# Two streams of 256 columns at the ends of a feed-forward stage

## The reference

```python
for l in range(DEPTH):
    h = x * (1 + sc1) + sh1
    hc = xc * (1 + sc1c) + sh1c
    y, yc = _token_mixers(h, hc, ...)          # attention; ends in "@ w_out"
    x = _layer_norm(ALPHA * x + g1 * y, ln1_g[l], ln1_b[l])
    h = x * (1 + sc2) + sh2
    x = _layer_norm(ALPHA * x + g2 * _sq_relu_mlp(h, w_fc1[l], w_fc2[l]), ln2_g[l], ln2_b[l])
    if not last:
        # the same three lines for the context: xc, yc, g1c, g2c ...
```

## Time and profile before

| | us |
|---|---|
| median of 3 runs (2049.69 to 2050.71) | 2050.25 |
| the profiled execution's own time | 2044.91 |
| its span, first to last instruction | 2043.1 |
| PE busy | 1857.0 |
| DVE busy | 1123.4 |
| mean granted TensorE clock | 0.958 |

### The profile page before, as it was taken

The page is one execution under the profiler, slowest core; times in us unless marked ns, Lnnn a source line. Parts: engine busy times, 40 slices in busy tenths (PEclk is TensorE's granted clock), DMA queues, the critical chain, the costliest instruction groups (busy, mean ns, idle before and its releaser), DMA issues.

```text
span 2043.1 us, 24319 instructions
## 1 busy us (share of the span) xinstructions
PE 1857.0 (91%) x9816; PEld 1322.5 (65%) x9816; DVE 1123.4 (55%) x1848; ACT 761.8 (37%) x1206; POOL 112.7 (6%) x152
## 2 busy tenths in 40 slices
PE   6998799999899899999988887999999788889996
PEld 5655555555576554557635556888888574579996
DVE  5662533323445422337457646788776765756665
ACT  2163333423242433334256534323222424645443
POOL 0770000000000000000000002000000100010000
PEclk9989899999999999999989998999999898989998
DMA  9778499999557899993210021354454031024440
GB/s 368 303 281 319 171 417 398 412 399 371 234 191 281 331 417 422 421 419 119 83 42 1 12 72 51 135 206 178 194 206 178 29 124 42 1 88 175 173 144 21
DMA packets 61848, 430.15 MB, mean 211 GB/s; under 512 B 6560, under 2 KB 9760, under 8 KB 9888
## 3 DMA queue, kind: packets, MB, share of 16 engines
q1 hardware_dynamic: 61728, 428.51, 53.0%
HBM read 427.43 MB, written 1.05 MB: 210 GB/s over the span
## 4 chain that ended last, share of the span: by engine, by line
PE 71%; DVE 17%; ACT 9%; issue 2%; DMA 0%; DVEq 0%; SPq 0%; POOL 0%; ACTq 0%
PE bank L293 14%; PE bank L1141 10%; PE bank L297 9%; PE bank L298 9%; PE bank L299 9%; PE bank L1129 7%; DVE ring_halves L2466 3%; ACT work_halves L2460 2%; PE bank L332 2%; ACT work_halves L1061 2%; DVE ring_halves L1068 2%; PE bank L2139 1%; PE bank L2116 1%; DVE work L439 1%; PE bank L2487 1%
## 5 line engine op out<-in xcount | busy, mean ns | idle before, releaser
L297 PE MATMUL bank<-work_halves 128*128 128x512 f32 (+1 forms) x1344 | 473.5, 352 | 37.9 <-DVE ring_halves L2466 12.1
L299 PE MATMUL bank<-work_halves,ring_halves 128*128 128x512 f32 (+1 forms) x1344 | 461.7, 343 | 0.0
L297 PEld LDWEIGHTS bank<-work_halves 128*128 128x128 f32 x1344 | 259.1, 193 | 76.3 <-DVE ring_halves L2466 15.1
L298 PE MATMUL bank<-HH_halves,work_halves 128*128 128x512 f32 (+1 forms) x832 | 289.8, 348 | 0.0
L299 PEld LDWEIGHTS bank<-work_halves,ring_halves 128*128 128x128 f32 x1344 | 258.8, 193 | 28.9
L1141 PE MATMUL bank<-ring,work 128*64 128x512 f32 x1024 | 261.2, 598 | 0.4 <-ACT work_halves L1324 0.4
L2466 DVE TENSOR_TENSOR ring_halves<-ring,work_halves 128x2048 fp32r<-128x2048 f32 x72 | 164.7, 2288 | 48.3 <-ACT work_halves L2460 48.3
L298 PEld LDWEIGHTS bank<-HH_halves,work_halves 128*128 128x128 f32 x832 | 162.2, 195 | 20.5 <-issue 2.2
L293 PE MATMUL bank<-HH,ring 128*128 128x256 f32 x704 | 160.2, 387 | 13.2 <-DVE HH L518 6.6
L298 PE MATMUL bank<-work_halves 128*128 128x512 f32 (+1 forms) x512 | 172.0, 336 | 0.0
L293 PEld LDWEIGHTS bank<-HH,ring 128*128 128x128 f32 x704 | 135.3, 194 | 42.5 <-issue 13.8
(11 more groups left out here) (322 smaller groups left out, 2629.7 us busy)
## 6 DMA issues: line engine op xcount, KB each, us to landing
ring<-in_ws_dram SPq DMA_DIRECT2D x380, 1024.0 KB, 7.3
work<-in_ws_dram SPq DMA_DIRECT2D x24, 1024.0 KB, 9.5
con<-in_con_dram SPq DMA_DIRECT2D x1, 1204.0 KB, 25.1
XX<-in_xT_dram SPq DMA_DIRECT2D x1, 1024.0 KB, 9.9
XX<-in_cT_dram SPq DMA_DIRECT2D x1, 1024.0 KB, 15.5
out_dram<-XX SPq DMA_DIRECT2D x1, 1024.0 KB, 4.8
par<-in_par_dram SPq DMA_DIRECT2D x1, 338.0 KB, 3.0
con<-in_con_dram SPq DMA_DIRECT2D x1, 128.0 KB, 2.9
```

Source lines behind the costliest of these rows:

```text
L297: pe.matmul(out, l[0], r[0], start=start, stop=False)
L298: pe.matmul(out, l[0], r[1], start=False, stop=False)
L299: return pe.matmul(out, l[1], r[0], start=False, stop=stop)
```

## The change

The 512 columns of layer 0's feed-forward stage are handled as two streams of 256 (the number q, 0 for the tokens and 1 for the context) at both ends of the stage. In the output projection PE runs all eight products for stream 0, then all eight for stream 1, and the norm of stream 0 is spread between the steps of stream 1 on ACT, DVE and PE. Fc1 0 (`pe_first`) runs over stream 0, then the variance matmuls of stream 1, then stream 1. Fc2 7 (`pe_last`) runs eight products for stream 0 and eight for stream 1, with the norm of stream 0 begun in between, and waits for both of its weight chunks before the first product. The first projection of layer 1's mixer runs over stream 0, then does the variance matmuls of stream 1, then runs over stream 1. The fourth weight chunk gets a buffer of its own, the evictions four buffers of 256 columns, and one buffer of the next mixer is placed elsewhere so that both of its first splits come at step 34. Layer 1's stage (one stream) goes through the same functions.

```diff
 class Mix:                                   # __init__
-    after = work[:, WORK - 2 * CW:WORK - CW]
+    after = work[:, 13312:13312 + CW] if self.last else work[:, WORK - 2 * CW:WORK - CW]
...
     def pe_proj(self, pe, *tiles):
...
-        for k in range(8):
-            for b, (name, w, m, n) in zip(bs, tiles):
-                for q in range(n // 256):
-                    st.wait_ge(pe, "xl", k, q)
...
+        streams = ((0, 1), (1, 2)) if self.before and len(tiles) > 1 else ((0, 2),)
+        for q0, q1 in streams:
+            if q0 > 0:
+                self.before.pe_norm(pe, 1, 1)
+            for k in range(8):
+                for b, (name, w, m, n) in zip(bs, tiles):
+                    x = slice(256 * q0, min(n, 256 * q1))
+                    if x.start >= n:
+                        continue
+                    for q in range(q0, x.stop // 256):
+                        st.wait_ge(pe, "xl", k, q)
...
+                    t = mm3(pe, b[:, x], (wh[:, k, c], wl[:, k, c]), (xh[:, k, x], xl[:, k, x]), k == 0, k == 7)
...
 class Ffn:
-    self.tmp = [work[:, 5120 + 512 * i:5632 + 512 * i] for i in range(2)]
+    self.tmp = [work[:, 5120 + 256 * i:5376 + 256 * i] for i in range(4)]
+    self.extra = work[:, 6144:8192]
...
+    def high_of(self, i):
+        return self.extra if i == 3 and self.nq == 2 else self.buf[i % 3]
...
+    def pe_norm(self, pe, v, q):
...
+        for k in range(0, 8, 2):
+            st.wait_ge(pe, "dev", v, q, k)
+            t = pe.matmul(b[:, 0:256], ones, self.dev[:, k, self.half(q)], start=k == 0, stop=k == 6)
...
+    def pe_sums(self, pe, v, q, o):
+        if o < 2 and q > 0:
+            self.pe_sum(pe, v, q - 1, 6 + o)
+        if o >= 2:
+            self.pe_sum(pe, v, q, o - 2)
+        if o == 7 and q == self.nq - 1:
+            self.pe_sum(pe, v, q, 6)
+            self.pe_sum(pe, v, q, 7)

     def pe(self, pe):
+        for q in range(self.nq):
+            for o in range(8):
...
+                b = bank_of(pe, st, self.ro, "out", q, o)
+                st.wait_ge(pe, "low", j)
+                for k in range(8):
+                    st.wait_ge(pe, "ol", k)
+                    t = mm3(pe, b[:, 0:256], (wh[:, k, c], wl[:, k, c]), (oh[:, k, x], ol[:, k, x]), k == 0, k == 7)
...
+                self.pe_sums(pe, 0, q, o)
+                if q > 0 and o == 4:
+                    self.pe_norm(pe, 0, 0)
...
-                    self.pe_fc1(pe, 0, (0, 1), i)
+                    self.pe_first(pe, i)
...
+                elif f < 7:
                     self.pe_fc2(pe, f, j, i)
+                elif j == 0:
+                    st.wait_ge(pe, "low", i + 1)
+                    self.pe_last(pe, i)
...
+    def pe_first(self, pe, i):
+        tiles = [(j, m, bank_of(pe, st, self.ro, "fc1", 0, 2 * j + m)) for j in range(2) for m in range(2)]
+        for q in range(self.nq):
+            if q > 0:
+                self.pe_norm(pe, 0, 1)
+            for k in range(8):
+                st.wait_ge(pe, "xl", k, q)
+                for j, m, b in tiles:
...
+    def pe_last(self, pe, i):
+        for q in range(self.nq):
+            for o in range(8):
+                b = bank_of(pe, st, self.ro, "fc2", 7, q, o)
+                for k in range(4):
...
+                self.pe_sums(pe, 1, q, o)
+                if q > 0 and o == 5:
+                    self.pe_norm(pe, 1, 0)

     def act(self, act):                      # after the first stream's eight act_out
+        if self.nq == 2:
+            for o in range(8):
+                self.act_out(act, 1, o)
+                if o < 2:
+                    self.act_squares(act, 0, 0, range(4 * o, 4 * o + 4))
+                if o == 4:
+                    self.act_root(act, 0, 0)
+                    self.split_act(act, 4)
+                if o == 6:
+                    self.split_act(act, 5)
+                if o >= 5:
+                    self.act_rows(act, 0, ((0, 1), (2, 3), (4, 5, 6, 7))[o - 5])
+        q = self.nq - 1
+        self.act_squares(act, 0, q, range(8))
...
+        self.act_root(act, 0, q)
+        self.act_rows(act, q, range(8))
...
-            if self.next and i >= 34:
-                st.wait_ge(act, "used", self.w[i - 1])
-                self.next.split_act(act, i - 34)
+            if self.next and i == 34:
+                st.wait_ge(act, "used", self.w[33])
+                self.next.split_act(act, 0)
+                self.next.split_act(act, 1)
...
+        for q in range(self.nq):
+            self.act_squares(act, 1, q, range(8))
+            self.act_root(act, 1, q)
+            for k in range(8):
+                st.wait_ge(act, "normed", 1, q, k)
+                if self.next:
                     self.next.high_x(act, k, q)
+                act.activation(XX[:, k, c], XX[:, k, c], ACT.Identity, ...)

     def dve(self, dve):
+        self.dve_mean(dve, 0, 0)             # mean and eight subtractions of stream 0
+        if self.nq == 2:
+            self.dve_out(dve, 1, (0, 1))
+            self.dve_pairs(dve, 0, 0)
+            self.dve_out(dve, 1, (2, 3, 4))
+            self.dve_root(dve, 0, 0)
+            self.dve_rows(dve, 0, (0, 1))
+            self.split_dve(dve, 4)
+            self.dve_out(dve, 1, (5,))
+            self.dve_rows(dve, 0, (2, 3))
+            self.dve_out(dve, 1, (6,))
+            self.dve_rows(dve, 0, (4, 5))
+            self.split_dve(dve, 5)
+            self.dve_out(dve, 1, (7,))
+            self.dve_rows(dve, 0, (6, 7))
+            self.dve_mean(dve, 0, 1)
...
+        for o in range(8):
+            self.dve_last(dve, 0, o)
+            if self.next and o in (1, 3):
+                self.next.split_dve(dve, o // 2)
+        self.dve_mean(dve, 1, 0)
+        if self.nq == 2:
+            for o in range(3):
+                self.dve_last(dve, 1, o)
+        self.dve_pairs(dve, 1, 0)
+        if self.nq == 2:
+            for o in range(3, 8):
+                self.dve_last(dve, 1, o)
+        for q in range(self.nq):
+            if q > 0:
+                self.dve_mean(dve, 1, q)
+                self.dve_pairs(dve, 1, q)
+            self.dve_root(dve, 1, q)
+            for k in range(8):
+                dve.tensor_tensor(XX[:, k, c], XX[:, k, c], self.rs[:, c], MUL)...
+                if self.next:
+                    self.next.dve_h(dve, k, q)
+                    if k > 0 and q == 0:
+                        self.next.low_x(dve, self.next.st.dve, k - 1, 0)
...
     def pool(self, pool):
+        for q in range(self.nq):
+            for k in range(8):
+                c = slice(512 * k + 256 * q, 512 * k + 256 * q + 256)
...
```

More of the change, by code:

```diff
@@ L2437, in plan @@
                 ro = self.ro = Rota(list(range(6)))
-                for o in range(8):
-                    ro.take("out", o)
-                    if o % 2:
-                        self.feed()
-                ro.take("var", 0)
+                for q in range(self.nq):
+                    for o in range(8):
+                        ro.take("out", q, o)
+                        if q == 0 and o % 2:
+                            self.feed()
+                for q in range(self.nq):
+                    ro.take("var", 0, q)
                 s = 0
@@ L2445, in plan @@
                     for j in range(2):
-                        for m in range(2 if name == "fc1" else 4):
-                            ro.take(name, f, 2 * j + m if name == "fc1" else 4 * j + m)
+                        if (name, f) == ("fc2", 7):
+                            if j == 0:
+                                for q in range(self.nq):
+                                    for o in range(8):
+                                        ro.take("fc2", 7, q, o)
+                        else:
+                            for m in range(2 if name == "fc1" else 4):
+                                ro.take(name, f, 2 * j + m if name == "fc1" else 4 * j + m)
                         self.feed()
@@ L2481, in pe_sum @@
-            def pe_sum(self, pe, v, o):
-                if o >= 0:
-                    st, n = self.st, self.n
-                    st.wait_ge(pe, "res", v, o)
-                    if v == 1 and o == 0:
-                        st.wait_ge(pe, "mu", 0)
-                    t = pe.matmul(bank[6][:, 0:n], ones, XX[:, o, 0:n], start=o == 0, stop=o == 7)
-                    if o == 7:
-                        t.then_inc(st.pe("sum", v), 1)
+                return [k8(r_(a), c) for a in (self.high_of(i), ring_of(self.w[i]))]
@@ new lines, in half, with pe_sum @@
+            def half(self, q):
+                return slice(256 * q, 256 * q + 256)
+            def pe_norm(self, pe, v, q):
+                st = self.st
+                b = bank_of(pe, st, self.ro, "var", v, q)
+                for k in range(0, 8, 2):
+                    st.wait_ge(pe, "dev", v, q, k)
+                    t = pe.matmul(b[:, 0:256], ones, self.dev[:, k, self.half(q)], start=k == 0, stop=k == 6)
+                t.then_inc(st.pe("var", v, q), 1)
```

(27 more changed lines are left out.)

256 lines of the change are left out of this document (122 added, 134 removed).

## The result

| | before | after |
|---|---|---|
| median of 5 runs each, us | 2049.69 (2044.88 to 2050.71) | 2061.25 (2060.1 to 2065.32) |
| ratio, 95% interval | | 1.0064 (1.0048 to 1.0079) |
| the profiled execution's span, us | 2043.1 | 2059.3 |
| mean granted clock | 0.958 | 0.956 |

What follows compares the result with a forecast made beforehand. PE was taken as the bound, losing time only where it stands or runs at half clock. Parts -2.4 + 4.4 + 3.6 gave +5.6 us; against the median 2050.25 that is 2055.9, say 2056, range 2049 to 2062.

Steps and rivals of the forecast that it cites:

- row 0: Output projection, stream 1: PE waits 0.8 us for the sum of row 0, which DVE adds after mean and subtractions.
- the second chunk: Layer 0's fc2 7: PE waits 3.3 us for chunk 35, which DVE splits behind all additions of fc2 6.
- the bare chains: Before the second streams of fc1 0 and the projection: root to POOL's first row, 4.3 us with nothing covering it.
- the wait for the last sum of the first norm: End of the output projection's stream 1: PE waits 3.3 us for row 7, held by DVE's queue.
- half-clock start: Slow PE start after a stall: 1.9 us priced for stalls over 4 us, half of that between 2.5 and 3.5.
- A: Layer 0, output projection to fc1 0: -2.4 us; gains 1.5 with all half-clock starts, 5.4 with none.
- B: Fc2 7 of layer 0 to layer 1's first norm of a projection: +4.4 us, bounds +2.7 and +6.7.
- C: Fc2 7 in layer 1: the same wait for chunk 35, no second stream to gain from; +3.6 us, bounds 2.65 and 4.6.
- The cover: Start of fc1 1: seven other chunks loaded ahead hide the later freeing of the ring's slots; put at nothing.
- That the clock holds: Rival: the clock holds in all stalls of up to 3.5 us; +2, 2052 us; chance 0.22.
- Everything late adds up: Rival: all short stalls cold, second streams' rows at 1.2 us instead of 0.95; 2062 us; chance 0.10.
- The faster rival: Rival: the mixer after fc2 7's tail takes up the late splits; -5.5, 2045 us; chance 0.08.

Runs made afterwards that it cites:

- The kernel with the filled stalls: The kernel after, with PE doing column sums of constants, result thrown away, in eight of its new stalls: median 2056.53 us, ratio 1.0028 to the kernel before.
- five single edits: Each alone on the kernel after: wait per chunk 2054.16, POOL held back 2059.36, DVE's order 2059.47, second variance inside first stream 2057.02, mixer's splits moved 2058.03 us.
- the four together: The kernel after with wait per chunk, DVE's order, variance inside the first stream and moved splits: median 2037.88 us, ratio 0.9951 to the kernel before.

## Why the prediction was right and wrong

It had the sign (0.66 on slower), and 2061.25 lies just inside its range of 2049 to 2062. The size was wrong: 5.6 us against 11.6 in the medians and 15.9 in the stretch itself, where its forecast was 3 to 10. That the time fell into the range is in part luck: 15.9 on top of the median it started from, 2050.25, would have been 2066.

- **Every stall stood where it was put, and all but one had its size.** PE waits 0.80 for row 0 (forecast 0.8), 3.26 for the second chunk (3.3), 2.30 in fc2 7's second stream (2.3), 3.05 before the projection (3), 4.54 and 4.53 at the bare chains (4.3), 2.87 in layer 1 (2.65). The exception is the wait for the last sum of the first norm: 4.99, where 3.3 was forecast.
- **What failed is the size of two kinds of terms.** With no half-clock start in the new stalls its three parts add up to nothing (-5.4 + 2.7 + 2.65), with all of them to +9.8 (-1.5 + 6.7 + 4.6); it took +5.6. The kernel with the filled stalls is 7.3 us slower than the one before where the prediction had nothing, and the half clock is worth another 8.6 where it had taken 5.6. So 3 of the 10.3 us that are missing are the price of the clock, and the larger part, 7.3, is in the waits and chains themselves: POOL's hold on DVE in A makes 2.1 of it, the chains of B 2.2, and a part stays open.
- **The price of the clock** was the term that it set too low for the short stalls. The prediction priced a stall between 2.5 and 3.5 us with half of a half-clock start, 0.95 us, and that of 2.3 with none. In the eight profiles whose stalls aren't filled (the kernel after twice, five single edits and the four together), 32 stalls of 2.29 to 3.26 us stand in the changed places, and behind 29 of them came a half-clock stretch: 6 of 6 at 2.3, 11 of 12 at 2.8 to 2.9, 12 of 14 at 3.0 to 3.3. (One of 2.18, where POOL was held back, was followed by none.) Behind 23 of the 29 the half clock lasted some 3.4 us, so that up to 1.7 are lost; behind the six of 2.83 and 2.84 before the mixer's sum it lasted 6.8, with further waits of PE in it. The three that held were one each of 2.87, 3.06 and 3.26 us. Nine in ten would have been the weight, not one in two, though these are a few places seen repeatedly and not 32 independent ones. It is argued and not shown which evidence misled it: the pause of 3.7 us at whose end the clock had only just fallen was read as a stall that may be free, though the 3.4 us behind it ran at 0.50. In part A it had too much: the two half-clock starts there were put at up to 3.9 together and gave back 2.8 (the 2.3 above and the 0.5 of the slower start).
- **A** was put at -2.4 and came out at +0.7 by fc1 1. The wait before the last sum was 4.99 and not 3.3: the queue of DVE was counted right, but with 0.7 us for POOL's hold, where it was 2.8. These 2.1 us are nearly all of the 2.2 between +0.7 and its -1.5 with all half-clock starts. (Its own steps give 1216.1 and not 1215.5 for PE's being ready, since the 0.8 us of the first wait was left out there; nothing hangs on it, as DVE sets the time.) With POOL held back, and the clock at 1.00 behind the shorter wait, fc1 1 starts at 98.6, 3.3 sooner than in the kernel before: that much was to be won.
- **B** was put at +4.4 and came out at +9.4. The bound with every start at half clock ("cold" in the prediction) was +6.7, and the kernel with filled stalls shows what it was without any: from PE's being ready for fc2 7 (1573.99, 407.5 behind its start) to the reciprocal 73.2 us, against 68.3 before, so +4.9, where the prediction's lower bound was +2.7. Of the missing 2.2 I can name 1.3: 0.2 in the chain before the projection's second stream (4.5 and not 4.3), 0.4 in that stream, whose rows come every 1.2 us instead of 0.95 (its 8.4 us for the stream held 1.0 more than such rows need), and 0.7 that was taken off because the same working came out late for the kernel before. That correction took the error of one order of work off the sum for another. Where the other 0.9 arise stays open, and so do the 0.6 us in the mixer behind B, to which the prediction gave nothing.
- **C** was put at +3.6 with 4.6 as its upper bound. It is 2.87 of stall and 1.7 of half clock, 4.5. The other 1 us of the 5.5 is the last variance: 2.95 us from its start to the reciprocal before, at a granted clock of 0.72, and 4.11 after, at 0.59. The code there is the same, so I put it down to the moment at which the clock falls.
- **The cover held.** Nothing at the start of fc1 1 waited for a load; the ring's slots, freed one stream later, cost nothing, as was said.
- **The rivals.** That the clock holds was given 0.22 and is refuted. "Everything late adds up", 2062 with 0.10, is nearest to what happened: all short stalls were followed by half clock, and the rows came at 1.2 us. But its sum of 12.6 doesn't have POOL's hold of 2.8 either. The faster rival failed where the prediction said it decides, at the two bare chains and right behind the projection. The kernel with the four edits, which removes the first of these chains and the late splits along with two other causes of stalls, is indeed faster.

## What to carry to other kernels

When one long pause is cut into several short ones, each of them can pay for its own half-clock start, as 29 of 32 did here: price stalls like these, of 2.3 us and more, with up to 1.7 us on top unless a row of the same length shows otherwise, and then look which can be removed for nothing. Price also what one engine's work does to its neighbour's: POOL's hold on DVE was a larger error in part A than the clock. Three of the four edits that did so here only changed an order, and the fourth put a wait where its operand is used; together they turned 16 us of loss into 10 of gain. And read an experiment of a few us by the time between two landmarks of its profile, since the start of the changed stretch moves by up to 8 us with what lies ahead.

## What the runs showed of the hardware

- **The clock falls at its own moments.** The same stall of 5.0 us before the same sum was followed by 3.2 us at half clock in one kernel and 6 in another; one of 3.26 by some 3.5 in most and by none in one (the row below, with the variance moved). The Trainium skill, in "TensorE: Matmul & The Clock Gate", What's actually happening, says of the start of a kernel that the number of matmuls at the lower clock is "run-variable". The stretches here, behind stalls in the middle of a kernel, agree: 3.2 us and 6 behind the same stall. So one edit's gain can come with 1.7 us that belong to another stall.

```profile
1570.00:1574.00 4.00, 4.00 (x34) 4.00 (x35) 1.57 (x4) 0.41 (x1) 0.00 (x0) 1.00 0.85 354
```

- **Column sums of constants hold it up.** With 4 to 15 of them in a wait the clock was at 1.00 in all eight windows shown.
- **POOL's hold on DVE** cost about 0.5 us for each of the DVE instructions shown, whether it was an addition (0.42 without POOL beside it, 0.96 with) or a split eight times as wide (2.29 and 2.83).
